# Six u tiles and eight dots a head in the ranking, eight u tiles behind the lots, and the first gates in a buffer of their own

## What is computed

```
q = (x @ wq).reshape(n, 8 heads, 2, 128)
s = einsum('nhpd,hpkd->nhpk', q, subkeys)          # 128 keys a half
s_top, i_top = top_k(s, 16)                        # per half
best_s, best_j = top_k(all 256 sums of pairs, 16)  # per head
expert = i_top[0] * 128 + i_top[1];  gate = softmax(best_s)
h = einsum('nd,nhkd->nhk', x, u[expert])           # u, v: 16384 rows of 1024
out = einsum('nhk,nhkd->nd', gate * gelu(h), v[expert])
```

## Time and profile before

| what | value |
|---|---|
| median of 3 runs | 2052.14 us (2048.4 to 2053.71) |
| profiled execution, its own time | 2059.33 us |
| span of that execution | 2057.6 us |
| TensorE busy | 1920.2 us, 93% of the span |
| VectorE busy | 1509.3 us, 73% |
| ScalarE busy | 764.6 us, 37% |
| GpSimd busy | 604.0 us, 29% |
| DMA | 416.58 MB, 202 GB/s over the span |
| mean granted TensorE clock | 0.954 |

### The profile page before, as it was taken

One profiled execution on the slowest core, in us unless ns is written; L12 is line 12 of the kernel. 1 busy time (PEld: TensorE's weight loads), 2 busy tenths in 40 slices (PEclk: granted clock), 3 DMA queues, 4 the chain that ended last, 5 costly groups with the idle time before them and its releaser, 6 DMA issues.

```text
span 2057.6 us, 33992 instructions
## 1 busy us (share of the span) xinstructions
PE 1920.2 (93%) x13250; PEld 1625.3 (79%) x13250; DVE 1509.3 (73%) x2841; ACT 764.6 (37%) x1113; POOL 604.0 (29%) x403
## 2 busy tenths in 40 slices
PE   5989998789989879999899999989999999999996
PEld 4978876348974349999899999977888878889995
DVE  6277994314536248999989999947788878878887
ACT  3222454542220033343346666533333333333332
POOL 2322344000000025575662222222222323234540
PEclk9988999896999989999999999999999999999998
DMA  3211232000004024565568888989999999989991
GB/s 126 72 62 42 93 107 77 1 14 30 4 25 182 0 104 157 178 200 163 183 233 300 316 317 311 323 291 350 349 368 356 345 354 360 359 304 315 340 328 62
DMA packets 173724, 416.58 MB, mean 202 GB/s; under 512 B 13952, under 2 KB 89216, under 8 KB 170384
## 3 DMA queue, kind: packets, MB, share of 16 engines
q1 hardware_dynamic: 119728, 256.16, 36.7%
q0 software_dynamic: 36864, 134.23, 18.0%
q10 hardware_dynamic: 16992, 24.26, 3.2%
HBM read 363.08 MB, written 51.51 MB: 201 GB/s over the span
## 4 chain that ended last, share of the span: by engine, by line
PE 46%; DVE 11%; DMA 4%; issue 1%; ACT 0%; POOL 0%; SPq 0%; ACTq 0%; DVEq 0%
PE ps L2019 23%; PE ps L1934 14%; PE ps L1938 7%; PE ps L1992 3%; DMA gates<-dense_gates 2%; DMA w_staged<-in_stream 1%; DVE gathered_rows L1552 1%; DMA coef<-parked_gelu 1%; DVE keys L2085 1%; DVE top_at L2068 1%; DVE top_at L2077 1%; DVE s_head L2071 1%; DVE best_at L2068 0%; DVE best_at L2077 0%; DVE cand L2071 0%
## 5 line engine op out<-in xcount | busy, mean ns | idle before, releaser
L2019 PE MATMUL ps<-w_hl,coef_hl 128*128 128x512 f32 x2304 | 544.7, 397 | 7.5 <-DVE coef_hl L2204 7.4
L2019 PEld LDWEIGHTS ps<-w_hl,coef_hl 128*128 128x128 f32 x2304 | 436.2, 190 | 109.1 <-DVE coef_hl L2204 9.4
L1934 PE MATMUL ps<-h_hl,w_hl 128*128 128x384 f32 (+1 forms) x2304 | 449.5, 347 | 15.3 <-DVE h_hl L2039 8.7
L1934 PEld LDWEIGHTS ps<-h_hl,w_hl 128*128 128x128 f32 x2304 | 408.9, 190 | 30.0 <-issue 9.1
L1542 POOL DMA_INDIRECT gathered_rows<-in_u_rows,pick_index x128 | 166.5, 1301 | 426.4 <-DVE pick_hidden L1552 346.2
L1542 POOL DMA_INDIRECT gathered_rows<-in_v,pick_index x128 | 161.8, 1264 | 278.5 <-DVE h_tok L1561 239.3
L1868 ACT ACTIVATE w_hl<-w_staged 128x1024 fp32r<-128x1024 f32 x143 | 152.0, 1063 | 243.2 <-PE ps L2019 155.1
L1938 PE MATMUL ps<-h_hl,w_hl 128*128 128x384 f32 (+1 forms) x1152 | 231.5, 342 | 6.8 <-POOL w_hl L1804 6.8
L1938 PEld LDWEIGHTS ps<-h_hl,w_hl 128*128 128x128 f32 x1152 | 204.3, 189 | 12.5 <-POOL w_hl L1804 7.5
L1804 POOL TENSOR_TENSOR w_hl<-w_staged,w_hl 128x1024 fp32r<-128x1024 f32 x64 | 159.7, 2515 | 50.1 <-ACT w_hl L1833 33.9
L2173 DVE TENSOR_TENSOR w_hl<-w_staged,w_hl 128x1024 fp32r<-128x1024 f32 x130 | 157.9, 1219 | 18.4 <-ACT w_hl L1868 18.4
(11 more groups left out here) (316 smaller groups left out, 2518.9 us busy)
## 6 DMA issues: line engine op xcount, KB each, us to landing
w_staged<-in_stream SPq DMA_DIRECT2D x132, 512.0 KB, 5.5
h1T<-in_v SPq DMA_DIRECT2D x66, 512.0 KB, 7.7
w_staged<-in_v SPq DMA_DIRECT2D x62, 512.0 KB, 7.2
dense_gates<-lot SPq DMA_DIRECT2D x24, 1024.0 KB, 4.9
gates<-dense_gates SPq DMA_DIRECT2D x16, 1536.0 KB, 14.3
w_staged<-in_w_in_t SPq DMA_DIRECT2D x40, 512.0 KB, 3.4
parked_gelu<-h1T ACTq DMA_DIRECT2D x102, 192.0 KB, 4.0
coef<-parked_gelu SPq DMA_DIRECT2D x102, 192.0 KB, 6.4
```

The source lines that it names most:

```text
L1934: nc.tensor.matmul(ps[:, bank, 0:width], w_hl[:, j % RING, 0, P * k:P * (k + 1)], h_hl[:, part, k, lo:SEQ], start=(k == 0 and part == 0), ...
L2019: last = nc.tensor.matmul(ps[:, 2 + 2 * t + half, :], coef_hl[:, k % HLS, c, P * t:P * (t + 1)], w_hl[:, s % RING, v, 512 * half:512 * (ha ...
```

## The change

- The ranking takes six u tiles a head in place of four, so a head is eight tiles. GpSimd makes the low halves of all of them and of the 16 between, 80 in all where it was 64.
- `DOTS_A_HEAD` is 8 in place of 3: eight gathers on GpSimd and eight dots on VectorE a head, 56 in seven heads in place of 21.
- Behind the lots stand eight u tiles in place of six, a dot each. 120 tiles are parked and 8 are fresh, where it was 102 and 26.
- With 112 dots made before the sums (75 before), the 144 dots and adds that are left are spread evenly over the first 125 sums: 1.152 a sum.
- The two gates buffers become two tensors. `gates0` has a place of its own, so that its first contents are read back in three parts: lots 0 to 15 after lot 17 is stored, lots 16 to 21 after lot 23, the last two behind the loads of the last parked u tiles. `gates_landed[0]` counts three reads where it counted one.

```diff
+EXPERTS_A_HEAD = 6
-PARKED = 4 * PEER_HEADS + BETWEEN + 2 * LOTS + 6
+PARKED = EXPERTS_A_HEAD * PEER_HEADS + BETWEEN + 2 * LOTS + 8
...
-    PER_HEAD = 6
+    PER_HEAD = EXPERTS_A_HEAD + 2
...
+    FIRST_GATES = {LOTS - 7: slice(0, LOTS - 8), LOTS - 1: slice(LOTS - 8, LOTS - 2)}
+    FIRST_READS = len(FIRST_GATES) + 1
...
-    DOTS_A_HEAD, DOTS_A_LOT, DOTS_BEHIND = 3, 2, 1
+    DOTS_A_HEAD, DOTS_A_LOT, DOTS_BEHIND = 8, 2, 1
...
-    A_PARKED = 1.1
-    BEFORE_FRESH = EARLY + int(A_PARKED * PARKED)
-    used_by = [EARLY + int(A_PARKED * (k + 1)) if k < PARKED else
-               min(2 * PICKS, BEFORE_FRESH + -(-(2 * PICKS - BEFORE_FRESH) * (k + 1 - PARKED) // (FRESH - HLS)))
-               for k in range(EXPERT_KEYS)]
+    used_by = [min(2 * PICKS, EARLY + -(-(2 * PICKS - EARLY) * (k + 1) // (EXPERT_KEYS - HLS))) for k in range(EXPERT_KEYS)]
...
+        gates0 = sb("gates0", [P, LOTS, LOOP * LOT])
...
-            gates = sb("gates", [P, 2, LOTS, LOOP * LOT], at=third)
+            gates1 = sb("gates1", [P, LOTS, LOOP * LOT], at=third)
+            gates = [gates0[:, :, :], gates1[:, :, :]]
...
+            def load_first_gates(lots):
+
+                for j in range(2):
+                    sp.wait_ge(lot_stored[j], 16 * (lots.stop // 2))
+                sp.dma_start(gates[0][:, lots], dense[lots, :, 0:LOOP * LOT].rearrange("l p k -> p l k")
+                             ).then_inc(gates_landed[0], 16)
...
+                if n in FIRST_GATES:
+                    load_first_gates(FIRST_GATES[n])
             load_from(FIRST_BEHIND + RING, QUERIES + PARKED)
-            for j in range(2):
-                sp.wait_ge(lot_stored[j], 16 * (LOTS // 2))
-            load_gates(0)
+            load_first_gates(slice(LOTS - 2, LOTS))
```

More of the change, by code:

```diff
@@ L1742, in load_gates @@
                     sp.wait_ge(weighed, LOOP * (i - 1))
[L1743 removed]
+                sp.dma_start(gates[i % 2], dense[:, :, LOOP * LOT * i:LOOP * LOT * (i + 1)].rearrange("l p k -> p l k")
                              ).then_inc(gates_landed[i % 2], 16)
+            def load_first_gates(lots):
[3 more added lines that the diff above has]
+                             ).then_inc(gates_landed[0], 16)
             def load_parked(k):
@@ L1848, in _ @@
                     r, m = j // PER_HEAD, j % PER_HEAD
-                    high(i * (2 * PER_HEAD) + (j + 3), j + 3, i * 3 + ((j + 3) // RING + 1))
+                    high(i * (2 * PER_HEAD) + (j + 3), j + 3, i * (2 * PER_HEAD // RING) + ((j + 3) // RING + 1))
                     if m < 2:
@@ L1963, in _ @@
                         scores(i, r)
-                    n = 4 * r + m - 2
-                    tile(s, j, tile_bank(n, False), DENSE, (w_low, s + 1), [(gelu_made, i * 8 + (n + 1))])
+                    n = EXPERTS_A_HEAD * r + m - 2
+                    tile(s, j, tile_bank(n, False), DENSE, (w_low, s + 1), [(gelu_made, i * (2 * EXPERTS_A_HEAD) + (n + 1))])
             low_of = lambda s: (w_low, s + 1) if s < BY_POOL else (late_low, s - BY_POOL + 1)
@@ L2192, in weigh @@
                 if k % LOOP == 0:
-                    dve.wait_ge(gates_landed[k // LOOP % 2], 16 * (k // LOOP // 2 + 1))
+                    reads = k // LOOP // 2 + (FIRST_READS if k // LOOP % 2 == 0 else 1)
+                    dve.wait_ge(gates_landed[k // LOOP % 2], 16 * reads)
                 if k < PARKED:
@@ L2199, in weigh @@
                 at = LOT * (k % LOOP)
-                v_.tensor_tensor(x, x, gates[:, k // LOOP % 2, :, at:at + LOT], ALU.mult).then_inc(weighed, 1)
+                v_.tensor_tensor(x, x, gates[k // LOOP % 2][:, :, at:at + LOT], ALU.mult).then_inc(weighed, 1)
             def low_coef(k):
@@ L2283, in lay_out @@
     wq, u = by_columns(v["peer_wq"][0]), by_columns(v["peer_u"][0].T)
-    order = [t for h in range(PEER_HEADS) for t in (wq[2 * h], wq[2 * h + 1], *u[4 * h:4 * h + 4])]
-    stream = np.concatenate([np.stack(order), u[4 * PEER_HEADS:]])
+    order = [t for h in range(PEER_HEADS) for t in (wq[2 * h], wq[2 * h + 1], *u[EXPERTS_A_HEAD * h:EXPERTS_A_HEAD * (h + 1)])]
+    stream = np.concatenate([np.stack(order), u[EXPERTS_A_HEAD * PEER_HEADS:]])
     named = {"ln_in_g": v["ln_in_g"], "ln_in_b": v["ln_in_b"], "mu": v["b_mu"][0], "b_gate": v["b_gate"][0],
```

10 lines of the change are left out of this document (5 added, 5 removed).

## The result

The changed kernel takes 2099.06 us (median of 4 runs, 2095.92 to 2102.88), the kernel before beside it 2052.93 (4 runs, 2048.4 to 2054.13): ratio 1.023, 95% interval 1.0205 to 1.0255. It is 46 us slower, where 24.5 were forecast; 2099 is 1 us above the end of the range. The profiled execution has a span of 2101.0 us, 43.4 more than before, and is divided here at four places that both traces have: the first query tile of head 1, the u tile at the first lot, the first sum, and the end of the sums for the first token tile. "Left over" is what remains of the difference when the tiles that moved are counted at TensorE's own pace.

A forecast was written before the change was run, and what follows sets the result against it. TensorE, busy 93% of the span, was taken as the bound, so only its waits count. Terms 0 - 9.0 + 26.5 + 5 - 3 + 5 = +24.5 us on the median 2052.14 gave 2077 us, range 2048 to 2098.

The forecast's parts named there:

- the early gates: Between lots and sums: reading 1.05 MB of gates after lot 17 relieves the later tile waits, -3 us (-6 to +2).
- The closed round: Ranking: eight gathers, GpSimd's make-up run and VectorE's blocked cast make rounds of 43.0 us against 37.70; five rounds, +26.5 us.
- the gates after the last head: Before the transposes: late picks and eight dots ahead of the softmax make TensorE wait, +5 us (0 to 15).
- the sums: Sums stage: gathers at 1.152 a sum instead of 1.1 ask more of the DMA engines, +5 us (0 to +10).
- Tiles moved: TensorE: expert tiles moved from the sums to the ranking and behind the lots cost the same there, 0 us.
- The old wait: End of the ranking: TensorE's loss to late low halves and the slower clock goes with longer heads, -9.0 us.
- A: Rival on the ranking: the round never closes, VectorE stays within 37.7 us a head; -9 us, 2043; chance 0.15.
- B: Rival on the ranking: round stays open, gathers outlast TensorE's stock by 2 us a head; +5 us, 2057; chance 0.13.
- D: Rival on the ranking: the round closes at once at full length, seven rounds of 45 us; +58 us, 2110; chance 0.08.
- C: Rival on the ranking: VectorE waits for one low half at a time, 40.9 us a head; +11 us, 2063; chance 0.18.
- The sign that I gave for being right: Start of the lots: some 80 us later than at 1077, or 58 if A is right.

The follow-up runs named there:

- e9: Changed kernel with gathers one behind each low half, first gates read once, and the last head's eight dots behind the softmax of the gates; 2052.69 us (ratio 1.0006).
- e7: Kernel before, with GpSimd waiting for the end of its own low half before the next; 2045.65 us (ratio 0.9987).
- e11: Kernel before with the changed table of due times alone, gathers left spread evenly over all 125 sums; 2088.59 us (ratio 1.0183).
- e8: Kernel before with the gates' buffer and the three early gates reads alone; 2055.36 us (ratio 1.0041).
- e4: Changed kernel without the gates' own buffer, first gates read once after the last lot; 2086.4 us (ratio 1.0167).
- e3: Changed kernel with its eight gathers a head issued one behind each low half instead of in a row; 2074.01 us (ratio 1.0128).
- e5: Changed kernel with gathers one behind each low half, first gates read once, last head's eight dots inside the softmax; 2066.02 us (ratio 1.0092).
- e6: Changed kernel, with GpSimd waiting for the end of its own low half before going on, gathers in a row; 2079.07 us (ratio 1.0146).
- e10: The kernel of e9 with GpSimd also waiting for its own low half before the next; 2052.01 us (ratio 1.0007).
- e2: Changed kernel with five gathers and dots a head in place of eight, the rest left to the sums; 2077.8 us (ratio 1.0155).
- e1: Changed kernel with three gathers and dots a head in place of eight, the rest left to the sums; 2098.98 us (ratio 1.0232).
- e12: Kernel before with eight gathers and dots a head in place of three, four u tiles a head as before; 2128.34 us (ratio 1.0378).

## Why the prediction was right in kind and too small

The step of the prediction that failed is *the early gates*: it took 1.05 MB moved behind lot 17 for a relief of 3 us, and that stretch lost 6.4. The closed round, the gates after the last head and the sums had the right sign and were each put too small, by 4.3, 4.5 and 6.0 us.

*Tiles moved, 0.* Right: e9 has all of them and equals the kernel before.

*The old wait, -9.0.* Right in kind: with three or five dots no low half is waited for in a 37.7 us head, and in e7 the wait is gone: with the gap the stretch is 9.1 us shorter. But the median gained only 2.5 us, inside its interval. The 9.0 is of one execution: over TensorE's pace the same ranking lost 9.0 us in the trace of e11 and 4.0 in that of e8 (277.4 in the table). So 9.0 may be more than this wait costs on average; that stays open.

*The closed round, +26.5.* The step holds, and its length was nearly right, in part by luck: I took 43.0 us, the three rounds are 43.6, 45.2 and 43.6, but two of its parts were off in opposite directions. The gathers took 13.0 (I had between 12.0 and 13.9); the run was five low halves and not six, 11.7 for 14.1; and the part after the cast 18.4 for 14.4, which is the contact with single low halves that I had named and left out of the working. What was off is the count, five rounds at an even 5.3. Heads 4 to 7 lost 10.9, 7.1, 6.3 and 6.3 us, as far as they can be separated, and head 3 lost 0.2, 30.8 in all: four rounds, each dearer than 5.3, since I had not counted the lower clock behind each wait, and the first with the longest wait, 7.73 us.

*The gates after the last head, +5.* Too small: from the last head to the lots 9.5 us go (2.96 for a low half, 2.08 before the transposes, the rest in matmuls at a lower granted clock, 0.95 in that window for 1.00 before). The ranking and the tiles between are then 40.3 us over TensorE's pace, for 31.5 in my sum; less the 9.0 of before this is the +31.3 of the table.

*The early gates, -3.* This step failed in its sign: +6.4, 9.4 us off and the largest miss. I saw the DMA engines 87% busy in the lots and took the other 13% as room for 1.05 MB at 353 GB/s, 3.0 us. The read took 8.7 us to land, and the two tile loads behind it on SP's queue landed 11.9 and 10.4 us after their issue for 6.0 and 6.8. They had little lead (ScalarE's waits of 7.15, 11.08 and 10.86 us), and the lots never got it back. The DMA engines were not full all that time: they moved 372 GB/s from 1380 to 1388 us and 79 from 1388 to 1392. So what counted was less the room than that these loads stood behind the read; whether the same read on another queue would cost less was not tested. e4 and e8 show the loss from both sides, and so do e3 and e5 (324.4 and 313.1). With one read the stretch is 312.9 where before with two more tiles would be 316.0, so the -3 came with the two tiles behind the lots and not with the early read.

*The sums, +5.* The size was about right: e3, e4, e5, e6, e9 and e10, with the same table, take 575.5 to 578.5, 4 to 7 us over 571.6 (646.5 less the tiles moved). The changed kernel's own trace shows 11.0. The 4 to 7 above those six traces I can't assign. They lie in the parked part (515.5 us to its first fresh tile, for 508.3 to 511.4), and the early reads are not it, since e3 and e6 have them too. The reason I gave, TensorE's pace as the likelier limit at 353 GB/s, is what e2 and e11 bear out for the kernel before. The Trainium skill, SBUF — State Buffer, section "A bandwidth-pool intuition that's wrong", has about 358 GB/s for one core; the trace of e2 shows 369 over 500 us, so here the measurement decides. The margin above before's rate is 4%, and e1 and e11 spend it.

*The rivals.* A and B are out: the round closed. D had the size of a round right (45) but not its onset; the first three heads do take 37.7. C, where VectorE waits for one low half at a time, is out for the cast, by its rows (9.05 and 7.58 us) and by e6, which is C made true by an edit and takes 17 us less by the ratios. For the two-input operations C's rule holds: in e5 they got in after one low half of an unbroken run. The Trainium skill, SBUF — State Buffer, section "Who interferes with whom", lets the engine that starts first hold the shared ports for its whole instruction. The trace agrees for the two-input operations, and for the cast where GpSimd has a gap between instructions (e6: at most 2.10 us, e7: 2.04); for low halves back to back the cast waited over three or more boundaries.

The sign that I gave for being right, lots that start some 80 us later, does not follow from my own terms, which give 89 (66.6 + 22.5); it was 92.6.

Over all: the profiled executions are 43.4 us apart, 18.9 more than forecast. Of these 8.8 lie in the ranking and between, 9.4 in the early gates and 6.0 in the sums, less 5.2 at the start, which is the scatter of single executions.

## What to carry to other kernels

When one engine feeds several others, compare the length of the closed round (its pause, the backlog it makes up, the consumer that this blocks) with the period of the stage: below it a round cost nothing here (e2), above it every period paid the difference (e12), and here splitting the pause into single steps (e3, ratio 1.0128) cost less than shortening it (1.0155 and 1.0232), since the gathers left out had to be made in the sums. After removing such a wait, look at what the late engine does next: here 11 to 14 us came up before the transposes until the dots went behind the gates. An average DMA share below 1 is no room for a transfer at a given place; ask what lead the loads behind it have there.
